# T1 of the second feed-forward product built by two DMAs instead of a VectorE subtraction, with other homes and order for the weight quarters

## What is computed

```
    hid = jax.nn.relu(rmsnorm(h, norm_mlp_g[i]) @ w_ff1[i])     # 512x1024 @ 1024x4096
    h = h + (hid * hid) @ w_ff2[i]                              # 512x4096 @ 4096x1024
    gate = jax.nn.sigmoid(rmsnorm(h, ple_norm_g[i]) @ w_ple_gate[i])
    h = h + gate * (p[i] @ w_ple_proj[i])
return rmsnorm(h, final_norm_g)
```

## Time and profile before

| | us |
|---|---|
| median of 3 runs | 742.61 (740.42 to 744.04) |
| the profiled execution | 744.04, span in the trace 742.3 |
| TensorE busy | 726.1 (98% of the span) |
| VectorE busy | 537.5 (72%) |
| ScalarE busy | 410.5 (55%) |
| GpSimd busy | 124.1 (17%) |
| feed-forward part, from the trace | 366 to 686 |

### The profile page before, as it was taken

The page is one execution under the profiler, slowest core; times in us unless marked ns, Lnnn a source line. Parts: engine busy times, 40 slices in busy tenths (PEclk is TensorE's granted clock), DMA queues, the critical chain, the costliest instruction groups (busy, mean ns, idle before and its releaser), DMA issues.

```text
span 742.3 us, 9979 instructions
## 1 busy us (share of the span) xinstructions
PE 726.1 (98%) x3972; PEld 623.7 (84%) x3972; DVE 537.5 (72%) x561; ACT 410.5 (55%) x521; POOL 124.1 (17%) x104
## 2 busy tenths in 40 slices
PE   8999999999999999999999999999999999999996
PEld 7888887778888888888899779987999789987784
DVE  4656795576768465555889995899588967999774
ACT  5624456653675753314766643683456626573875
POOL 1022000756546000001110011201110021000000
PEclk9999999999999999999999999999999999999999
DMA  9632322343232153219767388848976597937311
GB/s 331 187 101 83 99 86 87 113 154 103 85 131 97 57 198 114 72 58 268 189 150 213 74 258 168 205 116 239 196 182 168 138 252 162 240 60 257 112 58 57
DMA packets 49029, 109.85 MB, mean 148 GB/s; under 512 B 4796, under 2 KB 6488, under 8 KB 48984
## 3 DMA queue, kind: packets, MB, share of 16 engines
q1 hardware_dynamic: 38792, 79.83, 32.6%
q0 software_dynamic: 8960, 25.17, 18.4%
q10 hardware_dynamic: 1232, 4.23, 1.9%
HBM read 88.21 MB, written 4.23 MB: 125 GB/s over the span
## 4 chain that ended last, share of the span: by engine, by line
PE 55%; DVE 19%; DMA 12%; issue 8%; ACT 5%; POOL 1%; DVEq 0%; SPq 0%; ACTq 0%; POOLq 0%
PE acc L1640 15%; PE acc L1642 15%; PE acc L1641 15%; DVE ring_lo L1396 8%; DMA quarter<-quarter 8%; PE side L1705 3%; DMA quarter<-in_w_ff 3%; ACT ring_hi L755 2%; DVE quarter L1437 2%; PE side L1802 2%; DVE h L1492 2%; DVE fS_lo L1475 1%; DVE fA_raw L1454 1%; PE side L1769 1%; PE side L1809 1%
## 5 line engine op out<-in xcount | busy, mean ns | idle before, releaser
L755 ACT ACTIVATE ring_hi<-quarter 128x1024 fp32r<-128x1024 f32 x112 | 113.7, 1051 | 107.0 <-DMA quarter<-quarter 44.9
L1396 DVE TENSOR_TENSOR ring_lo<-quarter,ring_hi 128x1024 fp32r<-128x1024 f32 x112 | 132.7, 1220 | 40.2 <-ACT ring_hi L755 39.9
L1640 PE MATMUL acc<-w_hi,a_hi 128*128 128x512 f32 x256 | 104.4, 408 | 0.0
L1642 PE MATMUL acc<-w_hi,a_lo 128*128 128x512 f32 x256 | 100.0, 391 | 0.0
L1641 PE MATMUL acc<-w_lo,a_hi 128*128 128x512 f32 x256 | 99.7, 390 | 0.0
L1641 PE MATMUL acc<-xS_lo,ring_hi 128*128 128x256 f32 x256 | 72.4, 283 | 0.0
L1093 DVE TENSOR_TENSOR w_lo<-w_raw,w_hi 128x1024 fp32r<-128x1024 f32 x36 | 48.0, 1337 | 27.8 <-ACT w_hi L656 27.3
L635 POOL DMA_DIRECT2D quarter<-quarter x32 | 27.8, 868 | 183.7 <-DVE ring_lo L1396 136.3
L1640 PEld LDWEIGHTS acc<-w_hi,a_hi 128*128 128x128 f32 x256 | 48.1, 188 | 10.8 <-issue 1.4
L1641 PEld LDWEIGHTS acc<-w_lo,a_hi 128*128 128x128 f32 x256 | 48.2, 188 | 10.6 <-issue 1.4
L1642 PEld LDWEIGHTS acc<-w_hi,a_lo 128*128 128x128 f32 x256 | 48.0, 188 | 10.4
(11 more groups left out here) (290 smaller groups left out, 1833.0 us busy)
## 6 DMA issues: line engine op xcount, KB each, us to landing
quarter<-in_w_ff SPq DMA_DIRECT2D x64, 512.0 KB, 6.7
w_raw<-in_w_in SPq DMA_DIRECT2D x36, 512.0 KB, 3.8
quarter<-quarter POOLq DMA_DIRECT2D x32, 512.0 KB, 5.4
w_raw<-in_w_out SPq DMA_DIRECT2D x16, 512.0 KB, 3.4
quarter<-in_w_ff POOLq DMA_DIRECT2D x16, 512.0 KB, 7.9
h<-in_x SPq DMA_DIRECT2D x8, 512.0 KB, 4.4
seg<-cs_dram ACTq DMA_DIRECT2D x8, 512.0 KB, 3.9
w_raw<-in_w_ple_gate SPq DMA_DIRECT2D x8, 512.0 KB, 5.0
```

The costliest lines, as they stand in the source:

```text
L755: act.activation(ring[n % 3][0][at], quarter[i][at], ACT.Copy).then_inc(form_hi, 1)
L1396: dve.tensor_tensor(lo[at], src, hi[at].bitcast(F32), ALU.subtract).then_inc(form_lo, 1)
L1640: pe.matmul(dst, st[0], mv[0], start=start, stop=False)
L1642: return pe.matmul(dst, st[1], mv[0], start=False, stop=stop)
```

## The change

The second half's T1 isn't made by VectorE any more. After T3 has been split and T2's sum has landed, SyncE reads B12 of the second half once more into quarter1 (`reload_b12`), and GpSimd adds B11 to it from HBM with an accumulating DMA. `make_t1` stays for the first half. For that the homes of B21, B22 and T4 change to the same buffers in both halves (B21 and T4 in quarter2, B22 in quarter3), the order of SyncE's reads changes, and some waits with it. The two adds to h in unit 0 move from ahead of both(3) to behind both(9).

```diff
-    return {"B12": m, "T3": m, "T1": m, "B11": 1 - m, "T2": 1 - m, "B21": 3 - m, "T4": 3 - m, "B22": 2 + m}[name]
+    return {"B12": m, "T3": m, "T1": m, "B11": 1 - m, "T2": 1 - m, "B21": 2, "T4": 2, "B22": 3}[name]
...
-                        last_use = ("T1", "T2", "B22", "T4")[i]
+                        last_use = ("T1", "T2", "T4", "B22")[i]
                         sp.wait_ge(form_lo, form_count(u, 0, last_use, p))
                         if i == 1:
                             sum_landed(sp, u, 0, "T4", p)
-                            sp.wait_ge(t1_made, 4 * u + p + 1)
+                            sp.wait_ge(t1_made, 2 * u + p + 1)
                     elif u:
                         last_use = ("T2", "T1", "T4", "B22")[i]
                         sp.wait_ge(form_lo, form_count(u - 1, 1, last_use, p))
                         if i == 0:
                             sum_landed(sp, u - 1, 1, "T4", p)
-                            sp.wait_ge(t1_made, 4 * u - 1 + p)
...
+            def reload_b12(u):
+
+                for p in range(2):
+                    sum_landed(sp, u, 1, "T2", p)
+                    sp.wait_ge(form_lo, form_count(u, 1, "T3", p))
+                    k = 8 * u + 2 * p
+                    sp.dma_start(quarter[RELOAD][:, 2 * p:2 * p + 2, :], w_ff2[:, k:k + 2, 512:1024]
+                                 ).then_inc(q_landed[RELOAD][p], 16)
...
                 load_quarter(u, 1, "B12")
+                load_quarter(u, 1, "B21")
                 load_quarter(u, 1, "B11")
-                load_quarter(u, 1, "B21")
                 load_quarter(u, 1, "B22")
+                reload_b12(u)
                 if u < UNITS - 1:
-                    load_quarter(u + 1, 0, "B21")
                     load_quarter(u + 1, 0, "B12")
                     load_quarter(u + 1, 0, "B11")
                     load_quarter(u + 1, 0, "B22")
+                    load_quarter(u + 1, 0, "B21")
...
+                elif name == "T1":
+                    pool.wait_ge(q_landed[RELOAD][p], 16 * (3 * u + 3))
+                    k = 8 * u + 2 * p
+                    src = w_ff2[:, k:k + 2, 0:512]
...
-                    for name in ("T3", "T2", "T4"):
+                    for name in ("T3", "T2", "T1", "T4") if m else ("T3", "T2", "T4"):
...
-                    dve.wait_ge(xn_ready, 2 * NS)
-                    dve.tensor_tensor(h21, h21, h22, ALU.add).then_inc(h_added, 1)
-                    dve.tensor_tensor(h12, h12, h22, ALU.subtract).then_inc(h_added, 1)
...
                 both(9)
+                if u == 0:
+                    dve.wait_ge(xn_ready, 2 * NS)
+                    dve.tensor_tensor(h21, h21, h22, ALU.add).then_inc(h_added, 1)
+                    dve.tensor_tensor(h12, h12, h22, ALU.subtract).then_inc(h_added, 1)
...
-                for p in range(2):
-                    make_t1(u, 1, p)
                 both(11)
```

More of the change, by code:

```diff
@@ L28, in home @@
 def home(m, name):
-    return {"B12": m, "T3": m, "T1": m, "B11": 1 - m, "T2": 1 - m, "B21": 3 - m, "T4": 3 - m, "B22": 2 + m}[name]
-LOADS = ((("B12", 0), ("B11", 1)), (("B11", 0), ("B12", 1)), (("B22", 0), ("B21", 1)), (("B21", 0), ("B22", 1)))
-SUMMED = ((("T3", 0), ("T2", 1)), (("T2", 0), ("T3", 1)), (("T4", 1),), (("T4", 0),))
+    return {"B12": m, "T3": m, "T1": m, "B11": 1 - m, "T2": 1 - m, "B21": 2, "T4": 2, "B22": 3}[name]
+LOADS = ((("B12", 0), ("B11", 1)), (("B11", 0), ("B12", 1)), (("B21", 0), ("B21", 1)), (("B22", 0), ("B22", 1)))
+SUMMED = ((("T3", 0), ("T2", 1)), (("T2", 0), ("T3", 1), ("T1", 1)), (("T4", 0), ("T4", 1)))
+RELOAD = 1
 def build_layer(nc, a, out):
@@ L240, in build_layer @@
         q_landed = [[sem(f"q_landed{i}{p}") for p in range(2)] for i in range(4)]
-        t_landed = [[sem(f"t_landed{i}{p}") for p in range(2)] for i in range(4)]
+        t_landed = [[sem(f"t_landed{i}{p}") for p in range(2)] for i in range(3)]
         t1_made = sem("t1_made")
@@ L365, in quarter_count @@
             i = home(m, name)
-            return 16 * (len(LOADS[i]) * u + LOADS[i].index((name, m)) + 1)
+            per_unit = len(LOADS[i]) + (i == RELOAD)
+            return 16 * (per_unit * u + LOADS[i].index((name, m)) + 1)
         def sum_landed(eng, u, m, name, p):
@@ L541, in _ @@
                 if p < 2:
-                    sp.wait_ge(t1_made, 4 * UNITS)
                     for i in range(2):
@@ L746, in split_form @@
                     act.wait_ge(q_landed[i][p], quarter_count(u, m, name))
-                elif name == "T1":
-                    act.wait_ge(t1_made, 4 * u + 2 * m + p + 1)
+                elif name == "T1" and m == 0:
+                    act.wait_ge(t1_made, 2 * u + p + 1)
                 else:
@@ L1429, in _, with make_t1 @@
                         normed(1, s)
-            def make_t1(u, m, p):
+            def make_t1(u, p):
                 at = (slice(None), slice(2 * p, 2 * p + 2))
[L1434 to L1439, removed]
+                sum_landed(dve, u, 0, "T2", p)
+                dve.wait_ge(form_lo, form_count(u, 0, "T3", p))
+                dve.wait_ge(q_landed[3][p], quarter_count(u, 0, "B22"))
+                dve.tensor_tensor(quarter[0][at], quarter[1][at], quarter[3][at], ALU.subtract).then_inc(t1_made, 1)
             def combine(u, what):
@@ L1526, in _ @@
                     x_split("S2")
-                    dve.wait_ge(xn_ready, 2 * NS)
-                    dve.tensor_tensor(h21, h21, h22, ALU.add).then_inc(h_added, 1)
-                    dve.tensor_tensor(h12, h12, h22, ALU.subtract).then_inc(h_added, 1)
                 both(3)
                 for p in range(2):
-                    make_t1(u, 0, p)
+                    make_t1(u, p)
                 if u == 0:
```

## The result

The changed kernel is slower: 749.84 us median of 5 runs (747.99 to 752.37) against 742.61 (739.62 to 744.04), a ratio of 1.0109 with a 95% interval of 1.0072 to 1.0147. The forecast was 738.0 in a range of 735.5 to 742.4. The time lies outside it, on the other side of the kernel before: the case of a late B21, held to be worth 0.10 and 747.9, is what came, and it came 2 us dearer.

What follows compares the result with a forecast made beforehand. TensorE was taken to set the pace, losing time at B22 to VectorE's queue with make_t1. Gains of 3.32 (units 1 to 3) + 0.84 (unit 0) + 0.4 = 4.6 us gave 738.0 from 742.61, range 735.5 to 742.4.

Steps and rivals of the forecast that it cites:

- the case of a late B21: Rival at unit boundaries: the next unit's B21 lands late, 3.3 us lost at three boundaries, 747.9 us; chance 0.10.
- What bounds the kernel: Feed-forward part: TensorE sets the pace; its waits at B22 come from VectorE's queue with make_t1, 5.3 us lost in all.
- The reload and the T1 add in the hole: Second half: the new transfer pair falls where DMA share is 0.00; cost 0, cover 7 us.
- 3.3 for units 1 to 3: B22 of the second half: its losses go whole without make_t1, 0.79 + 1.25 + 1.28 = 3.32 us.
- Unit 0: With the moved adds, T2's product starts 0.6 us later, and B22's earlier start wins 0.84 us.
- 2.03 against 0.84: Unit 0 at B22: with the two h adds moved, it wins 0.84 us, not 2.03.
- with 6.7 for the read: Next unit's B21: read taken at 6.7 us after form T4, ready at 524.6 where TensorE wants it at 530.6.
- cost 0, cover 6.0 us: B21's new place in the next unit's reads: no loss at its product, 6.0 us to spare.
- the rival: The late B21 at three unit boundaries: decides from a landing of 12.7 us on, 747.9 us; chance 0.10.
- T3's adds start earlier: Next unit's reads: T3's adds go 4 us earlier, T2's behind them; cited against the late B21.
- The first rival: Second half: gain eaten on VectorE as both(7) or both(9) slips, units 1 to 3 win 0.6, 742.0 us; chance 0.12.

Runs made afterwards that it cites:

- moved_adds_alone: The kernel before with only unit 0's two adds to h moved behind both(9): 743.71 us against 740.83 (ratio 1.0043).
- t1_by_dma_alone: The kernel before with only the second half's T1 made by reload and accumulating DMA, without make_t1 there: 737.37 us (ratio 0.9921).
- t2_held: The changed kernel, with GpSimd issuing T2's adds of the next unit's first half only after B21 has landed: 747.22 us in one run.
- b21_third: The changed kernel with B21 ahead of B22 in the next unit's reads: 740.60 us (ratio 0.9977).
- new_homes_mended: The changed kernel with B21 ahead of B22 in the next unit's reads and B11 ahead of B21 in the second half's: 739.16 us.
- homes_only: The kernel before with the new homes and read order; VectorE makes T1, with no reload or T1 add: 755.29 us (ratio 1.0205).

## Why the prediction was wrong

- **What bounds the kernel: right.** The loss ahead of B22 was VectorE's queue with make_t1 in it. The profile's "issue" was resolved correctly from the ends of the rows: with make_t1 gone, all four losses went. In unit 1 h_add T2 had 2.45 us to spare where 1.59 was worked out (S4's sum started without its pause, as forecast); over the four units it is 1.1 to 2.5. What the prediction did not see is that the loss needs this pause as well (moved_adds_alone).
- **The reload and the T1 add in the hole: right.** t1_by_dma_alone, which is this part by itself, gained 5.0 us by the medians; with 3.3 for units 1 to 3, 2.0 for unit 0 without the moved adds and 0.4, the forecast's own terms say 5.7.
- **Unit 0: right.** T2's product lost 1.46 against 0.76, 0.7 where 0.6 was forecast; B22 came 0.58 sooner after the first product, where 0.84 was forecast. Here the adds at their new place do what was forecast; that they are better left where they were, the forecast's own 2.03 against 0.84 already said.
- **The step that failed: "with 6.7 for the read" of B21, "cost 0, cover 6.0 us".** The time of issue was right: 519.43, and less the 4.55 that TensorE was late by then 514.9, against 514.4. The landing was not. The median of 64 reads was put on one whose place in the queue is the last and which has T2's adds beside it: it took 12.5 to 17.3. So a term given as cost 0 was a gap of 3.8, 0.9 and 3.9 us. The kernel before had B22 in that place, needed so late that no wait spoke of it. Its DMA issues at the third boundary (start, then landing in us):

```profile
L516 SPq DMA_DIRECT2D quarter<-in_w_ff x2: 367/368/368, 595.7 to 596.8; - x2
...
DMA to landing us min/median/max: 7.6/9.6/11.6
```

The later of the two took 8.4, 9.2 and 11.6 at the three boundaries. So the place makes a read slower than the median of its line, but these rows alone would still have kept the landing under the 12.7 from which the rival decided. Of the rest, 2 to 5 us are what the change itself put beside the read (the next point). What makes the remainder, 11.2 to 12.0 with T2's adds held back against medians of 7.4 to 9.6 for the last two reads in the kernel before, no run tells. The row's maximum of 16.0 stood in the prediction as a bound and went into the rival, but the rival's chance was taken from the median.
- **"T3's adds start earlier" was put down against the late B21.** It was for it. T3's adds were indeed earlier (the first one issued at 512.66, less the same 4.55, so 508.1 against 516.59), and T2's adds with them, which brought these into the time of B21's read. t2_held shows the 2 to 5 us that this cost. The Trainium skill, DMA: Bandwidth & Descriptors, section Issuing engines are not separate DMA queues, states that the transfers of both engines run on the same 16 DMA engines and interleave. The trace agrees by these numbers; the prediction followed the rule only into the rival.
- **The rival's price missed the clock.** 3.3 us at three boundaries was forecast, 3.8, 0.9 and 3.9 came as gaps, 8.6 against 9.9. The 5.1 us of slow matmuls (2.6, 0.1 and 2.4) were in no term.
- **The first rival (B21 ahead of B11 delays both(7)) is real,** but it did not show in the changed kernel. That the gaps at the boundary gave VectorE the time there is argued, not shown; b21_third, without these gaps, uncovered it: 0.6 to 1.7 us a unit, where 0.9 had been put down.

So one edit gains (T1 by DMA, 5.0 by the medians) and three lose: B21 last among the next unit's reads (most of it: 13.7 by the bill above, 9.2 by the medians of the changed kernel and b21_third, where the next one comes out), B21 ahead of B11 (seen only once the first is mended; 1.4 between b21_third and new_homes_mended), and the moved adds (1.3, 1.6 and 2.9 by three pairs of medians). The homes neither gain nor lose.

What stays open is why the granted clock stayed up behind gaps of 2.7 and 0.9 us and fell behind one of 2.2 in moved_adds_alone. There the product before (T3's) had run with 512 columns a matmul, in the others B11's with 256. No run tells these apart.

## What to carry to other kernels

When a change moves a transfer to another place in a queue, read the landing of the transfer that stands in that place now, not the median of its line (8.4 to 11.6 us here against 6.7), and then add what the change puts beside it: one that nobody waits for can be slow without leaving a wait in the profile. Work that starts earlier than before isn't only cover; ask beside which transfer it now runs. And a gap on TensorE of some microseconds may cost a third to three quarters as much again in slow matmuls behind it (the gaps of 3.1 to 5.0 us here), so price it by a row of such a gap if there is one. Last, a wait at the end of an engine's queue can need two things at once, a long queue and a late start of it; look at both before you say what removing one of them is worth.

## What the runs showed of the hardware

- The clock of TensorE was granted at 0.50 behind gaps of 3.1 to 5.0 us at a unit boundary, in four kernels, and stayed at 1.00 behind those of 0.5 to 2.7 there. The slow stretch cost 1.5 to 2.6 us each time. Behind a gap of 2.2 us ahead of T2's product it fell too (moved_adds_alone, 1.5 us). With no gap TensorE was kept busy for 314 us at 1.00.
- The same read of B21 (medians of its two halves of 512 KB) took 4.3 to 4.9 us as the first of the unit's reads, in the kernel before; 9.4 to 10.7 behind B12 and B11, with T2's accumulating DMAs beside its end (b21_third); 11.2 to 12.0 behind B22 too, with T2's held back (t2_held); and 13.5 to 16.7 with both (changed kernel), 12.8 to 13.5 in homes_only.
- A DMA share of 0.86 over the whole feed-forward part left TensorE without a wait; the mean share says little, and what counts is what lands last at each place.
